# Post-expert and pre-mixer normalisations of a two-layer backbone: from three passes with a barrier to a pipeline over tiles

## What is computed

```python
def _layer_norm(x, g=None, b=None):
    mu = xf.mean(-1, keepdims=True)
    var = jnp.square(xf - mu).mean(-1, keepdims=True)
    y = (xf - mu) * lax.rsqrt(var + LN_EPS)
    if g is not None: y = y * g + b
...
    ml = _expert_choice_ffn(hl, ...)
    xl = _layer_norm(alpha * xl + g2 * ml, ln2_g[l], ln2_b[l])     # end of layer l
    ...
    hl = _layer_norm(xl) * (1.0 + sc1) + sh1                       # start of layer l + 1
    yl, yc = _token_mixing(hl, hc, ...)
```

## Time and profile before

| | us |
|---|---|
| median of three runs | 3771.17 |
| lowest, highest | 3766.63, 3771.34 |
| profiled execution | 3768.74 |
| its span, first to last instruction | 3766.7 |
| TensorE busy (share of the span) | 3401.9 (90%) |
| VectorE busy | 2276.4 (60%) |
| ScalarE busy | 1621.1 (43%) |
| POOL busy | 615.1 (16%) |

### The profile page before, as it was taken

One profiled execution on the slowest core, in us unless ns is written; L12 is line 12 of the kernel. 1 busy time (PEld: TensorE's weight loads), 2 busy tenths in 40 slices (PEclk: granted clock), 3 DMA queues, 4 the chain that ended last, 5 costly groups with the idle time before them and its releaser, 6 DMA issues.

```text
span 3766.7 us, 49816 instructions
## 1 busy us (share of the span) xinstructions
PE 3401.9 (90%) x19108; PEld 2788.2 (74%) x19108; DVE 2276.4 (60%) x3357; ACT 1621.1 (43%) x2095; POOL 615.1 (16%) x480
## 2 busy tenths in 40 slices
PE   7998899899999969999997399998999969999994
PEld 4997678888887857777775288678766657788873
DVE  3696741511111649999997684742332257999997
ACT  3114742411110237777774322753211127777762
POOL 2001012212121012221211200112222101111110
PEclk9999999999999979999998599998999979999997
DMA  7332133022222329999997122121123217999994
GB/s 248 101 137 94 46 102 124 13 73 73 74 90 78 104 89 336 328 326 334 335 338 258 58 90 79 51 91 46 52 89 101 85 74 280 350 344 362 357 341 173
DMA packets 331923, 632.85 MB, mean 168 GB/s; under 512 B 14526, under 2 KB 104910, under 8 KB 325358
## 3 DMA queue, kind: packets, MB, share of 16 engines
q1 hardware_dynamic: 309056, 557.88, 42.4%
q0 software_dynamic: 22704, 72.68, 5.8%
HBM read 614.00 MB, written 16.50 MB: 167 GB/s over the span
## 4 chain that ended last, share of the span: by engine, by line
PE 71%; DVE 13%; ACT 6%; issue 4%; DMA 4%; DVEq 0%; POOL 0%; ACTq 0%; SPq 0%; POOLq 0%
PE ps L851 43%; PE ps L1265 17%; DVE part L2092 2%; PE ps L981 2%; PE ps L1013 2%; ACT hx L1536 2%; DVE area L1696 1%; PE ps L999 1%; DMA raw<-in_w_exp_gate 1%; ACT area L1388 1%; PE ps L1001 1%; DMA raw<-in_w_exp_up 1%; DVE area L2100 1%; ACT area L1315 1%; DVE stat L1606 1%
## 5 line engine op out<-in xcount | busy, mean ns | idle before, releaser
L851 PE MATMUL ps<-hx,part 128*128 128x384 f32 (+2 forms) x4704 | 929.4, 356 | 11.1 <-POOL part L518 5.5
L851 PEld LDWEIGHTS ps<-hx,part 128*128 128x128 f32 x4704 | 830.3, 189 | 98.6 <-issue 23.2
L1265 PE MATMUL ps<-part,hx 128*128 128x512 f32 x3072 | 752.1, 398 | 16.6 <-ACT part L1536 11.0
L1265 PEld LDWEIGHTS ps<-part,hx 128*128 128x128 f32 x3072 | 578.3, 191 | 149.2 <-ACT part L1536 12.7
L2092 DVE TENSOR_TENSOR part<-raw,part 128x2048 fp32r<-128x2048 f32 x256 | 593.2, 2319 | 100.4 <-ACT part L1536 99.2
L1536 ACT ACTIVATE part<-raw 128x2048 fp32r<-128x2048 f32 x256 | 490.2, 1916 | 157.2 <-PE ps L1265 88.9
L1265 PE MATMUL ps<-hx 128*128 128x512 f32 x1536 | 382.6, 398 | 8.9 <-ACT hx L1536 7.2
L518 POOL TENSOR_TENSOR part<-raw,part 128x2048 fp32r<-128x2048 f32 x52 | 237.9, 4575 | 821.2 <-ACT part L515 821.2
L1265 PEld LDWEIGHTS ps<-hx 128*128 128x128 f32 x1536 | 290.0, 190 | 81.7 <-ACT hx L1536 11.0
L851 PE MATMUL ps<-part,hx 128*128 128x256 f32 (+2 forms) x2208 | 315.0, 305 | 18.3 <-DVEq L532 15.5
L2092 DVE TENSOR_TENSOR hx<-raw,hx 128x2048 fp32r<-128x2048 f32 x128 | 295.9, 2311 | 57.8 <-ACT hx L1536 56.2
(11 more groups left out here) (256 smaller groups left out, 3706.0 us busy)
## 6 DMA issues: line engine op xcount, KB each, us to landing
raw<-in_w_exp_gate SPq DMA_DIRECT2D x128, 1024.0 KB, 5.7
raw<-in_w_exp_up SPq DMA_DIRECT2D x128, 1024.0 KB, 5.9
raw<-in_w_exp_down SPq DMA_DIRECT2D x128, 1024.0 KB, 6.5
raw<-in_w_mod SPq DMA_DIRECT2D x48, 1024.0 KB, 6.0
raw<-in_w_in SPq DMA_DIRECT2D x44, 1024.0 KB, 5.5
raw<-in_w_gate SPq DMA_DIRECT2D x32, 1024.0 KB, 7.9
area<-in_bias POOLq DMA_DIRECT2D x32, 512.0 KB, 4.0
raw<-in_w_branch SPq DMA_DIRECT2D x16, 1024.0 KB, 7.2
```

The lines of the kernel that those rows point to most:

```text
L851: last = mm(dst, a, b, start=i == 0, stop=i == len(pairs) - 1)
L1265: last = mm(ps[:, bank, :], x, y, start=kh == 0 and a == 0, stop=kh == 1 and a == len(pairs) - 1)
```

## The change

The closing of layer 0 and the normalisation ahead of layer 1 become one loop of nine steps on VectorE and ScalarE, in which step `s` holds different parts of the tiles `s`, `s - 1`, `s - 2` and `s - 3`. The variance comes from ScalarE (Square with the negative mean as bias and an accumulated sum, then Sqrt with epsilon as bias), the sums for the means from accumulating VectorE passes. The closing's affine is `(x - mean) * g` and then `* 1/std + b`. The second normalisation is one Identity op of ScalarE into one of two `xhat2` buffers, transposed by TensorE as each is ready. The barrier behind the normalisation is gone; POOL loads the parameters, makes the two low parts, and then stores the tiles to `x_d`; ScalarE waits for these stores ahead of the A/B copies. The last layer closes in the same two parts, a tile's second part behind the next tile's first.

```diff
 POOL
@@ -660,7 +662,10 @@
                 pool.wait_ge(*S("params_in", l).at(64))
                 if l:
-                    st.leave()
+                    split.mixers_to(l, 2)
+                    for t in range(NT):
+                        pool.wait_ge(*S("x2", l).at(t + 1))
+                        load(x_d[t], x2v[:, t, :]).then_inc(*S("x_out", l).by(16))
                 else:
@@ -807,12 +812,11 @@
-                for t in range(full):
-                    pool.wait_ge(*S("x2", l).at(t + 1))
-                    dst = x_d[t] if l < DEPTH - 1 else out[0, t * P:(t + 1) * P, :]
-                    load(dst, x2v[:, t, :]).then_inc(*S("x_out", l).by(16))
-                pool.wait_ge(*S("x_out", l).at(16 * full))
                 if l == DEPTH - 1:
+                    for t in range(full):
+                        pool.wait_ge(*S("x2", l).at(NT + t + 1))
+                        load(out[0, t * P:(t + 1) * P, :], x2v[:, t, :]).then_inc(*S("x_out", l).by(16))
+                    pool.wait_ge(*S("x_out", l).at(16 * (NT + full)))
                     st.leave()
 TensorE
@@ -900,14 +904,15 @@
                     turn_modt(8 * KD)
-                    st.leave()
                 for t in range(NT):
+                    if l:
+                        pe.wait_ge(*S("xhat_n", l).at(t + 1))
                     if t >= 2:
                         pe.wait_ge(*S("h_tmp", l).at(t - 1))
                     for k in range(KD):
...
+                        src = xhat2[:, t % 2, k * P:(k + 1) * P] if l else xhat[:, t, k * P:(k + 1) * P]
+                        last = nc.tensor.transpose(psf[:, t % 2 * D + k * P:t % 2 * D + (k + 1) * P], src, ident)
 ScalarE
@@ -1302,12 +1307,23 @@
-                for t in range(NT):
+                for t in range(NT if l == 0 else 0):
...
-                if l:
-                    st.leave()
+                def deviation(t, mean, square, dev, done):
+                    sf = stat[:, t % 4, :]
+                    own(fn(psf[:, 6 * 512:8 * 512], x2v[:, t, :], ACT.Square, bias=sf[:, mean:mean + 1],
+                           accum_out=sf[:, square:square + 1]))
+                    own.wait()
+                    fn(sf[:, dev:dev + 1], sf[:, square:square + 1], ACT.Sqrt, bias=eps_c[:, 0:1], scale=1.0 / D
+                       ).then_inc(*done.by(1))
+                def closing(t, base):
+                    act.wait_ge(*S("q_mu", l).at(base + t + 1))
+                    deviation(t, 1, 2, 3, S("q_std", l))
@@ -1316,19 +1332,38 @@
+                else:
+                    split.mixers_to(l, 2)
+                    for s in range(NT + 3):
+                        if s >= 3:
+                            modulated(s - 3)
+                        if 1 <= s <= NT:
+                            act.wait_ge(*S("x2", l).at(s))
+                            deviation(s - 1, 6, 10, 7, S("v_std", l))
+                        if 2 <= s <= NT + 1:
+                            t, sf = s - 2, stat[:, (s - 2) % 4, :]
+                            act.wait_ge(*S("v_nb", l).at(t + 1))
+                            if t >= 2:
+                                act.wait_ge(*S("xhat_T", l).at(t - 1))
+                            fn(xhat2[:, t % 2, :], x2v[:, t, :], ACT.Identity, bias=sf[:, 9:10], scale=sf[:, 8:9]
+                               ).then_inc(*S("xhat_n", l).by(1))
+                        if s < NT:
+                            closing(s, 0)
@@ -1374,6 +1409,8 @@
+                if l:
+                    act.wait_ge(*S("x_out", l).at(16 * NT))
                 copies("ab_part", AB_GROUPS, S("ab_out", l), 3, turn=2)
@@ -1571,10 +1608,9 @@
-                for t in range(full):
-                    act.wait_ge(*S("q_var", l).at(t + 1))
-                    fn(stat[:, 0, 15:16], stat[:, 0, 14:15], ACT.Sqrt).then_inc(*S("q_std", l).by(1))
                 if l == DEPTH - 1:
+                    for t in range(full):
+                        closing(t, NT)
 VectorE
@@ -1653,17 +1689,61 @@
-                else:
-                    take_modt(0, 4)
-                    st.leave()
...
+                def negative_mean(sf, total, mean):
+                    own.wait()
+                    return V.tensor_scalar(sf[:, mean:mean + 1], sf[:, total:total + 1], -1.0 / D, None, ALU.mult)
+                def close_sum(t, base):
+                    x, a, sf = x2v[:, t, :], acc[:, t, :], stat[:, t % 4, :]
+                    own(V.tensor_tensor(a, a, rows2[:, t // TL, :], ALU.mult))
+                    own.wait()
+                    own(V.scalar_tensor_tensor(x, x, ALPHA, a, ALU.mult, ALU.add, accum_out=sf[:, 0:1]))
+                    negative_mean(sf, 0, 1).then_inc(*S("q_mu", l).by(1))
+                    dve.wait_ge(*S("q_mu", l).at(base + t + 1))
+                    own(V.scalar_tensor_tensor(a, x, sf[:, 1:2], rows2[:, 2, :], ALU.add, ALU.mult))
+                def close_norm(t, base):
+                    x, a, sf = x2v[:, t, :], acc[:, t, :], stat[:, t % 4, :]
+                    dve.wait_ge(*S("q_std", l).at(base + t + 1))
+                    own(V.reciprocal(sf[:, 4:5], sf[:, 3:4]))
+                    own.wait()
+                    return V.scalar_tensor_tensor(x, a, sf[:, 4:5], rows2[:, 3, :], ALU.mult, ALU.add, accum_out=sf[:, 5:6])
...
+                    for s in range(NT + 3):
+                        if 1 <= s <= NT:
+                            own(close_norm(s - 1, 0))
+                            negative_mean(stat[:, (s - 1) % 4, :], 5, 6).then_inc(*S("x2", l).by(1))
+                            dve.wait_ge(*S("x2", l).at(s))
+                        if 2 <= s <= NT + 1:
+                            sf = stat[:, (s - 2) % 4, :]
+                            dve.wait_ge(*S("v_std", l).at(s - 1))
+                            own(V.reciprocal(sf[:, 8:9], sf[:, 7:8]))
+                            own.wait()
+                            V.tensor_tensor(sf[:, 9:10], sf[:, 6:7], sf[:, 8:9], ALU.mult).then_inc(*S("v_nb", l).by(1))
+                        if s == 2:
+                            take_modt(0, 4).then_inc(*S("modc_done", l).by(1))
+                        if s < NT:
+                            close_sum(s, 0)
+                        if s >= 3:
+                            low_part(s - 3)
@@ -2160,18 +2240,14 @@
...
+                    for t in range(full + 1):
+                        if t < full:
+                            close_sum(t, NT)
+                        if t:
+                            close_norm(t - 1, NT).then_inc(*S("x2", l).by(1))
```

More of the change, by code:

```diff
@@ L148 @@
 e_yH e_yL e_comb var std conv_sig conv_cent conv_var conv_std conv_normed m_abs m_log m_exps m_gate
[L149 removed]
+p_var p_std z_gate r_cent r_exp e_sil q_mu q_std v_std v_nb xhat_n conv_part ab_part d_part ab_out d_out
 merge_part out_part ya_out ya_in yc_out yc_in conv_tapped x1_out x1_in pt_in0 pt_in1
@@ L451, in build @@
         rows2, _ = cut(ys, NT * D, 4, D)
-        stat = sb("stat", [P, 2, 18])
+        stat = sb("stat", [P, 4, 18])
+        eps_c = sb("eps_c", [P, 1])
+        xhat2, _ = cut(ys, 10 * D, 2, D)
         stage = S("stage_done")
@@ L1317, in modulate, with modulated @@
                     last.then_inc(*done.by(1))
-                if l:
-                    split.mixers_to(l, 2)
-                for u in range(NT):
-                    if l == 0:
-                        split.mixers_to(l, max(u - 3, 0))
+                def modulated(u):
                     act.wait_ge(*S("xhat_T", l).at(u + 1))
-                    if l == 0 and u == 0:
+                    if u == 0:
                         act.wait_ge(*S("modc_done", l).at(1))
@@ L1331, in _ @@
                     fn(h_hi[:, :, u * P:(u + 1) * P], htmp[:, u % 2, :, :], ACT.Copy).then_inc(*S("h_hi", l).by(1))
+                if l == 0:
+                    for u in range(NT):
+                        split.mixers_to(l, max(u - 3, 0))
+                        modulated(u)
+                else:
[15 more added lines that the diff above has]
+                            closing(s, 0)
                 pa = conv_parts(l)
@@ L1588, in _ @@
                 if l == 0:
+                    own(V.memset(eps_c[:, :], EPS))
                     dve.drain().then_inc(S("split_v"), RING)
@@ L1618, in _ @@
                     dve.wait_ge(*S("x_in", l).at(16 * NT))
-                else:
-                    dve.wait_ge(*S("x2", l).at(0))
-                for t in range(NT):
+                for t in range(NT if l == 0 else 0):
                     own(standardise(xall[:, t, :], xhat[:, t, :], stat[:, t % 2, :], S("var", l), S("std", l), t + 1))
@@ L1655, in _, with low_part @@
                     last.then_inc(*S("modc_done", l).by(1))
-                else:
-                    take_modt(0, 4)
-                    st.leave()
-                for u in range(NT):
-                    if l == 0 and u == 1:
-                        move_mod(0)
+                def low_part(u):
                     dve.wait_ge(*S("h_hi", l).at(u + 1))
```

(29 more changed lines are left out.)

6 lines of the change are left out of this document (2 added, 4 removed).

## The result

Six runs of the changed kernel gave a median of 3739.07 us (3733.15 to 3744.80), six of the kernel before beside them 3770.39; the ratio is 0.9915, 95% interval 0.9904 to 0.9926. The forecast was 3739.5 us in a range of 3728 to 3753, faster. The profiled execution took 3737.83 us over a span of 3736.2, 30.5 less than the span of before.

What follows compares the result with a forecast made beforehand. Bound: a VectorE-then-ScalarE chain at the layer boundary, and VectorE at the end. Profiled 3768.74 us less 30.0 (19.3 and 10.7 gained) is 3738.7; with 0.8 allowed, 3739.5 us, range 3728 to 3753.

Steps and rivals of the forecast that it cites:

- both places: Boundary from layer 0's first closing op to layer 1's first conv, 19.3 us gained; last closing at kernel end, 10.7 gained.
- VectorE per tile: Boundary steps: VectorE's sum, normalisation, small ops and low_part together take 7.4 us a tile.
- ScalarE per tile: Boundary steps: modulated, two deviations and xhat2 take 8.2 us a tile, making ScalarE the bound of steady steps.
- Charged 8.4: Boundary steps 1 and 2: POOL's two weight splits hold VectorE's passes, 8.4 us of their 9.0 on the path.
- The memset at zero: Boundary: POOL's memset of cpad, 2.9 us, comes when VectorE has slack and costs zero.
- The steps: Boundary pipeline worked through in order: conv starts 70.2 us after the first closing op instead of 89.35.
- Step 2's root: Boundary: ScalarE's closing in step 2, worked out to be done at 28.3 us, or 19.9 without POOL.
- The first (no hold): Rival at the boundary: POOL's splits do not hold VectorE; gain 8.4 us more, 3731 us; chance 0.16.
- the second: Rival at both deviation places: Square in another table set than Sqrt, two loads per deviation; 3761 us; chance 0.07.
- third: Rival in ScalarE's steps 2 to 7: every change of function reloads, six loads a step; 3775 us; chance 0.03.
- The fourth: Rival in the steps: engine hand-overs or accumulating passes cost more, 1 to 2 us a step; 3745 to 3753; chance 0.12.
- fifth: Rival at the boundary: closing and normalisation stay in sequence, only end and dropped passes gain; 3755 to 3766; chance 0.04.

Runs made afterwards that it cites:

- runs 3 and 4: Changed kernel with, at the boundary, each ScalarE Square made twice (3) or one more VectorE pass per tile (4): 3748.05 and 3743.81 us, one execution each.
- run 8: Changed kernel with ScalarE making xhat2 of a tile ahead of the next tile's second deviation, and in step 7 ahead of modulated(4): 3737.07 us, ratio 0.9894.
- run 1: Changed kernel with POOL's two layer 1 weight splits behind the last x_d store instead of ahead of the first: 3730.24 us, ratio 0.9884.
- run 9: On top of run 8, VectorE makes the two layer 1 weight splits in steps 6 and 7, POOL none: 3728.70 us, ratio 0.9879.
- run 11: On top of Run 10, the second normalisation's pass made by VectorE as tensor_scalar instead of ScalarE's Identity: 3723.23 us, ratio 0.9865.
- Run 10: On top of run 9, a [128,1] Sqrt opens ScalarE's boundary work and its two splits follow closing(0) and closing(1): 3719.36 us, ratio 0.9863.
- run 7: Changed kernel with a [128,1] Exp ahead of every ScalarE Square at the boundary, forcing table switches: 3770.55 us in one run.
- run 5: Changed kernel's work without overlapping its halves: all six tiles closed first, then second deviation, xhat2 and modulated tile by tile: 3741.49 us, ratio 0.9921.
- run 6: run 5 with a barrier of the four engines between the last tile's closing and ScalarE's second half: 3749.10 us, one execution.

## Why the prediction was right, point by point

*What bounds the kernel.* Right in both places: 21.8 and 11.9 us gained where 19.3 and 10.7 were worked out, and nothing gained elsewhere. The mechanism came as forecast. That the forecast of 3739.5 came within half a microsecond of the 3739.07 measured is luck: 3.7 us more were gained in the two places than worked out, and 3.1 were lost outside them.

*VectorE per tile.* The pass with an accumulating sum was taken at 1.25 us plus 0.08; the rows after say 1.22 or 1.28 and 0.08. The sum of a tile was charged a little too high: at the end the tiles go by in 5.3 us (3719.89 to 3725.20), not 5.63. A full wait was charged at every op, but the rows show ops that overlap: the accumulator read behind a pass starts some 0.1 us before the pass's end, and the next tile's pass, which does not depend on it, starts with it (both at 3725.20). Four times 0.3 is the 1.2 us of the end.

*ScalarE per tile.* The two deviations are 1.46 and 1.57, not 1.6 each, and `xhat2` 1.13, not 1.2; the wait for transposes is 0.60 and not half a microsecond, and starts in the second steady step, as the prediction had it. 7.96, 8.67 and 8.66 measured, 8.2, 8.7 and 8.7 worked out. That ScalarE is the bound was shown by runs 3 and 4, and that its waits for transposes are on the path by run 8.

*POOL.* Charged 8.4; 4.17 and 3.93 us over the plain passes, 8.1, and runs 1 and 9 gave back 7.8 and 7.7. Both held passes were scalar_tensor_tensor with two inputs in SBUF, and run 1 holds a tensor_tensor as well; both agree with the rule of the Trainium skill (SBUF — State Buffer, "Who interferes with whom"). The memset at zero: right here, where only tensor_tensor passes ran beside it, and run 11 shows that it hung on that. The same page of the Trainium skill says that a VectorE pass with two SBUF inputs contends only with a GpSimd instruction that reads SBUF, while forms that can go over both port pairs, tensor_scalar among them, can contend with GpSimd when they do. Run 10 agrees with the first half (1.22 and 2.29 us beside the memset) and the 4.01 us of run 11, the one case here, with the second.

*The steps.* Step 2's root was ready at 26.6 us instead of 28.3, from the cheaper small ops and 0.4 us on POOL's side; all behind it is 2 us early, to the conv at 68.0 instead of 70.2. The terms that were mis-sized, then, are small ones that add up: the charge of a full wait at every op of VectorE, worth 1.2 us at the end, and at the boundary, together with the first root (0.3 us early), POOL's hold (8.1 for 8.4) and ScalarE's ops, 2.2 us. How the 2.2 divide among them was not separated by a run. What hid them in the total is that 3.1 us were lost outside both places.

*The rivals.* The first (no hold) falls by the rows of 5.40 and 5.21 us and by run 1, the second and third (table loads) by the single load at L1321; run 7 prices the second at 24.1 us of conv distance where 20.6 had been worked out. The fourth and fifth left no trace, and run 5 says that the fifth was priced far too high: with the halves in sequence the time is 3741.49 us, with the barrier too 3749.10 (run 6), and not 3755 or more. What the prediction did not ask is what part of the boundary's gain comes from the pipeline itself. Taking away one thing after another, run 5 gives 4.2 us for the interleaving as it was built, net of the bare transposes that come with its order, and run 6 gives 6.4 for the barrier. The other 10.8 us (89.35 less 78.6) are what is left, and no run divides them: passes taken off VectorE, loads of POOL's that no longer wait for its stores, and against these POOL's 8.1.

## What to carry to other kernels

Before interleaving two engines' work by hand, add up each engine's work per tile: here ScalarE had 8 us a tile in any order, and the interleaving as built gave 4 us where dropped passes and the dropped barrier gave the rest. Then look at what each order leaves bare: with the transposes covered the same interleaving was worth 12. When a stage is shortened, look again at who else runs in it: POOL's two splits moved under VectorE's busiest steps and took 8 us back. Making them later, where VectorE has slack, gave that back whether POOL made them (run 1, 7.8 us) or VectorE itself (run 9, 7.7 us); which of the two is better on top of run 8's order was not tried. In a pipeline over engines, put each step whose result a third engine must turn around (here the transposes) first among the work that can cover it.

## What the runs showed of the hardware that was not expected

- A barrier behind a DMA issue of POOL: 3.1 us from the last issue (2097.03 + 0.53) to the release, though nobody waits for the store; the barrier cost 6.4 us where 3.5 had been worked out from what it keeps apart.
- One and the same memset of POOL (2.88 us) held a VectorE tensor_scalar for 3.2 us (4.01 less 0.81; seen once) and did not hold tensor_tensor passes of 2.29 and 1.22 us.
- Changing the function table between Exp and Sqrt cost the load of 1.28 us each time, with no drain in the rows; Square took no load of its own behind Exp or behind Sqrt.
